# Down and output products of a split-float32 transformer kernel: two products merged into one stream of 512 columns

## The reference

```python
for l in range(DEPTH):                       # first block
    h = h + 0.5 * swiglu(rmsnorm(h, g0), ...)
    h = h + mixer(rmsnorm(h, g1), ...)       # ... return y @ w_out
    h = h + 0.5 * swiglu(rmsnorm(h, g2), ...)  # (silu(x@w_gate)*(x@w_up)) @ w_down
for l in range(DEPTH):                       # second block
    ...
    x = x + g1 * (merged @ w_out[l])
    h2 = rms_norm(x, ln2_g[l]) * (1.0 + sc2) + sh2
    x = x + g2 * (jnp.square(jax.nn.relu(h2 @ w_ff1[l])) @ w_ff2[l])
```

## Time and profile before

| | |
|---|---|
| median of 3 runs | 1894.01 us (1892.62 to 1894.32) |
| the profiled execution's own time | 1892.72 us |
| its span in the trace | 1891.4 us |
| PE busy | 1863.0 us, 98% of the span, 15225 matmuls |
| DVE busy | 1348.1 us, 71% |
| ACT busy | 1045.7 us, 55% |
| the chain that ended last | PE 94%, DVE 3%, ACT 2% |

### The profile page before, as it was taken

The page is one execution under the profiler, slowest core; times in us unless marked ns, Lnnn a source line. Parts: engine busy times, 40 slices in busy tenths (PEclk is TensorE's granted clock), DMA queues, the critical chain, the costliest instruction groups (busy, mean ns, idle before and its releaser), DMA issues.

```text
span 1891.4 us, 36376 instructions
## 1 busy us (share of the span) xinstructions
PE 1863.0 (98%) x15225; PEld 1821.5 (96%) x15225; DVE 1348.1 (71%) x2298; ACT 1045.7 (55%) x1764; POOL 1.3 (0%) x8
## 2 busy tenths in 40 slices
PE   7999999999999999999999999999999999999998
PEld 6999998899999999999889999999999999999998
DVE  5777666577776777667658777698877558787744
ACT  6444575655444544456566544576566457656643
POOL 0000000000000000000000000000000000000000
PEclk9999999999999999999999999999999999999999
DMA  6777343346786577733334878445455554455553
GB/s 245 275 260 267 120 137 110 108 161 221 262 295 221 177 261 269 267 124 129 112 118 173 301 268 300 159 158 170 164 193 184 180 176 169 160 175 182 187 190 112
DMA packets 51810, 365.91 MB, mean 193 GB/s; under 512 B 6620, under 2 KB 8060, under 8 KB 9920
## 3 DMA queue, kind: packets, MB, share of 16 engines
q1 hardware_dynamic: 51648, 363.59, 54.5%
HBM read 362.52 MB, written 1.05 MB: 192 GB/s over the span
## 4 chain that ended last, share of the span: by engine, by line
PE 94%; DVE 3%; ACT 2%; issue 1%; DMA 0%; SPq 0%; DVEq 0%; ACTq 0%
PE bank L441 28%; PE bank L442 27%; PE bank L443 27%; PE bank L477 2%; PE bank L473 1%; PE bank L474 1%; DVE w_lo L1541 1%; PE bank L712 1%; PE bank L640 1%; ACT w_hi L1022 1%; DVE full L1583 1%; PE bank L697 0%; PE bank L742 0%; PE bank L646 0%; DVE xn_lo L1547 0%
## 5 line engine op out<-in xcount | busy, mean ns | idle before, releaser
L441 PE MATMUL bank<-xn_hi,w_hi 128*128 128x272 f32 (+2 forms) x2624 | 758.8, 289 | 1.0 <-DVE w_lo L1541 1.0
L443 PE MATMUL bank<-xn_lo,w_hi 128*128 128x272 f32 (+2 forms) x2624 | 746.0, 284 | 0.0
L442 PE MATMUL bank<-xn_hi,w_lo 128*128 128x272 f32 (+2 forms) x2624 | 746.0, 284 | 0.0
L441 PEld LDWEIGHTS bank<-xn_hi,w_hi 128*128 128x128 f32 x2624 | 494.1, 188 | 8.9 <-issue 5.9
L442 PEld LDWEIGHTS bank<-xn_hi,w_lo 128*128 128x128 f32 x2624 | 494.0, 188 | 1.1
L443 PEld LDWEIGHTS bank<-xn_lo,w_hi 128*128 128x128 f32 x2624 | 494.8, 189 | 0.0
L1541 DVE TENSOR_TENSOR w_lo<-raw_b,w_hi 128x1024 fp32r<-128x1024 f32 (+1 forms) x282 | 356.6, 1265 | 145.6 <-ACT w_hi L1022 145.1
L1541 DVE TENSOR_TENSOR w_lo<-raw_a,w_hi 128x1024 fp32r<-128x1024 f32 (+1 forms) x282 | 356.3, 1265 | 140.7 <-ACT w_hi L1022 139.7
L1022 ACT ACTIVATE w_hi<-raw_a 128x1024 fp32r<-128x1024 f32 (+1 forms) x282 | 307.0, 1090 | 260.5 <-PE bank L443 221.9
L1022 ACT ACTIVATE w_hi<-raw_b 128x1024 fp32r<-128x1024 f32 (+1 forms) x282 | 306.9, 1089 | 250.3 <-PE bank L443 225.7
L441 PE MATMUL bank<-h_hi,w_hi 128*128 128x272 f32 (+1 forms) x704 | 201.8, 287 | 0.0
(11 more groups left out here) (322 smaller groups left out, 2718.3 us busy)
## 6 DMA issues: line engine op xcount, KB each, us to landing
raw_a<-in_weights SPq DMA_DIRECT2D x123, 1024.0 KB, 4.8
raw_b<-in_weights SPq DMA_DIRECT2D x123, 1024.0 KB, 4.8
ada_raw<-in_ada_w SPq DMA_DIRECT2D x48, 1024.0 KB, 4.9
raw_a<-in_weights SPq DMA_DIRECT2D x16, 1408.0 KB, 5.9
raw_b<-in_weights SPq DMA_DIRECT2D x16, 1408.0 KB, 5.9
c_rows<-in_c_rows SPq DMA_DIRECT2D x3, 512.0 KB, 3.7
raw_a<-in_weights SPq DMA_DIRECT2D x2, 768.0 KB, 4.1
raw_b<-in_weights SPq DMA_DIRECT2D x2, 768.0 KB, 4.2
```

The lines of the kernel that those rows point to most:

```text
L441: pe.matmul(o, wh, xh, start=start, stop=False)
L442: pe.matmul(o, wl, xh, start=False, stop=False)
L443: return pe.matmul(o, wh, xl, start=False, stop=stop)
```

## The change

Where 256 token columns are live, the high and the low activations of one group are read as one moving operand of 2 x 256 columns (`pair`), in a matmul by the high weights that fills a whole bank: `wh*xh` in its columns 0 to 255 and `wh*xl` in columns 256 to 511. The product by the low weights goes to the first half. Both halves are added to `x` by DVE, one after the other. This is done in the last down product of the first block (176 products), the output of its second mixer (64), the outputs of both mixers of the second block (128) and both `w_ff2` (512): 880 products and 48 output tiles. The other stages keep three matmuls. For the pair to be one operand, a high and its low tile are now two parts of one allocation.

```diff
-            return sb(name + "_hi", [P, tiles, width], F32R, 256, 0), sb(name + "_lo", [P, tiles, width], F32R, 256, 128)
+            n = tiles * width
+            part = (n + 31) // 64 * 64 + 32
+            both = sb(name, [P, 2, part], F32R, 256, 0)
+            hi, lo = (both[:, i, 0:n].rearrange("p (k t) -> p k t", k=tiles) for i in range(2))
+            return hi, lo, lambda kk, cols: both[:, :, kk * width + cols.start:kk * width + cols.stop]
...
+    def product_apart(b, wh, wl, pair, start, stop):
+
+        pe.matmul(bank[b][:, 0:2 * N], wh, pair, start=start, stop=False, skip_group_check=True)
+        return pe.matmul(bank[b][:, 0:N], wl, pair[:, 0, :], start=False, stop=stop, skip_group_check=True)
...
+    def tiles_apart_as_ready(u, b0, pair, stage):
...
+        for kk in range(KD):
+            pe.wait_ge(*k.at("x_lo", (*stage, kk)))
+            s = slice(kk * P, (kk + 1) * P)
+            for b, (wh, wl) in enumerate((wa, wb)):
+                m = product_apart(b0 + b, wh[:, s], wl[:, s], pair(kk, TN), kk == 0, kk == KD - 1)
...
-                            m = product(bank[b][:, 0:N], wh[:, s], wl[:, s], c.f_hi[:, kf, :], c.f_lo[:, kf, :], kf == 0, kf == KF2 - 1)
+                            m = product_apart(b, wh[:, s], wl[:, s], c.f_pair(kf, TN), kf == 0, kf == KF2 - 1)
...
+                if live == TB:
+                    dve.tensor_tensor(c.x[:, m, live], c.x[:, m, live], bank[m % 4][:, N:2 * N], ALU.add).then_inc(*k.up("tile_v"))
+                    dve.wait_ge(*k.newest("tile_v"))
                 dve.tensor_tensor(c.x[:, m, live], c.x[:, m, live], bank[m % 4][:, packed(live)], ALU.add).then_inc(*k.up("tile_v", ("res", l, m)))
...
-                dve.scalar_tensor_tensor(out=c.x[:, m, TB], in0=bank[m % 4][:, 0:N], scalar=c.mod_all[:, l, 16 + m:17 + m], in1=c.x[:, m, TB],
-                                         op0=ALU.mult, op1=ALU.add).then_inc(*k.up("tile_v", ("res2", l, m)))
+                for half in (slice(N, 2 * N), TN):
+                    dve.scalar_tensor_tensor(out=c.x[:, m, TB], in0=bank[m % 4][:, half], scalar=c.mod_all[:, l, 16 + m:17 + m], in1=c.x[:, m, TB],
+                                             op0=ALU.mult, op1=ALU.add).then_inc(*k.up("tile_v", ("res2", l, m) if half == TN else None))
+                    if half != TN:
+                        dve.wait_ge(*k.newest("tile_v"))
```

More of the change, by code:

```diff
@@ L251, in __init__ @@
         place = shared
-        self.y_hi, self.y_lo = streamed("y", KD)
+        self.y_hi, self.y_lo, self.y_pair = streamed("y", KD)
         place = block_start
         shared = place
-        self.f_hi, self.f_lo = streamed("f", KF2, N)
+        self.f_hi, self.f_lo, self.f_pair = streamed("f", KF2, N)
         place = shared
@@ L269, in __init__ @@
         self.cq, self.ckv = self.cq_x[:, :, TN], self.ckv_x[:, :, TN]
[L270 to L271 removed]
+        self.cq_hi, self.cq_lo, _ = streamed("cq", 3, N)
+        self.ckv_hi, self.ckv_lo, _ = streamed("ckv", 2, N)
         self.k_rot = sb("k_rot", [96, N])
@@ L505, in leading_units, with tile_apart @@
                 tile(u + i, i, TX, c.xn_hi, c.xn_lo)
+    def tile_apart(u, b, pair):
+        take(b)
+        wh, wl = weights(u)
+        for kk in range(KD):
+            s = slice(kk * P, (kk + 1) * P)
+            m = product_apart(b, wh[:, s], wl[:, s], pair(kk, TN), kk == 0, kk == KD - 1)
+        end_unit(u, m)
+    def tiles_apart_as_ready(u, b0, pair, stage):
+        take(b0)
+        take(b0 + 1)
+        wa, wb = weights(u), weights(u + 1)
+        for kk in range(KD):
+            pe.wait_ge(*k.at("x_lo", (*stage, kk)))
+            s = slice(kk * P, (kk + 1) * P)
+            for b, (wh, wl) in enumerate((wa, wb)):
+                m = product_apart(b0 + b, wh[:, s], wl[:, s], pair(kk, TN), kk == 0, kk == KD - 1)
+                if kk == KD - 1:
+                    end_unit(u + b, m)
     def half_tiles(u, bs, cols, xh, xl, ready=()):
@@ L806, in mixer @@
                 if u == 42:
-                    tiles_as_ready(u0 + u, 0, packed(live), c.y_hi, c.y_lo, ("y", l))
+                    if live == TB:
+                        tiles_apart_as_ready(u0 + u, 0, c.y_pair, ("y", l))
+                    else:
+                        tiles_as_ready(u0 + u, 0, live, c.y_hi, c.y_lo, ("y", l))
                 free[u - 42] = [("tile_v", ("res", l, u - 42))]
@@ L810, in mixer @@
                 b = (u - 42) % 4
-                tile(u0 + u, b, packed(live), c.y_hi, c.y_lo)
+                if live == TB:
+                    tile_apart(u0 + u, b, c.y_pair)
+                else:
+                    tile(u0 + u, b, live, c.y_hi, c.y_lo)
                 free[b] = [("tile_v", ("res", l, u - 42))]
@@ L986, in mixer2 @@
                 if at == 39:
-                    tiles_as_ready(u, 0, TN, c.y2_hi, c.y2_lo, ("y2", l))
+                    tiles_apart_as_ready(u, 0, c.y2_pair, ("y2", l))
                 elif at > 40:
-                    tile(u, b, TN, c.y2_hi, c.y2_lo)
+                    tile_apart(u, b, c.y2_pair)
                 free[b] = [("tile_v", ("res2", l, at - 39))]
@@ L1714, in ffn @@
                     dve.wait_ge(k.sem["unit_done"], u + 1)
+                    if to == TN:
+                        dve.scalar_tensor_tensor(out=c.x[:, m, cols], in0=bank[b][:, N:2 * N], scalar=0.5, in1=c.x[:, m, cols], op0=ALU.mult,
+                                                 op1=ALU.add).then_inc(*k.up("tile_v"))
+                        dve.wait_ge(*k.newest("tile_v"))
                     dve.scalar_tensor_tensor(out=c.x[:, m, cols], in0=bank[b][:, to], scalar=0.5, in1=c.x[:, m, cols], op0=ALU.mult,
@@ L2120, in ff @@
                 dve.wait_ge(k.sem["unit_done"], u + 1)
-                dve.scalar_tensor_tensor(out=c.x[:, m, TB], in0=bank[4 + j][:, 0:N], scalar=c.mod_all[:, l, 40 + m:41 + m], in1=c.x[:, m, TB],
-                                         op0=ALU.mult, op1=ALU.add).then_inc(*k.up("tile_v", ("x2", l, m)))
+                for half in (slice(N, 2 * N), TN):
+                    dve.scalar_tensor_tensor(out=c.x[:, m, TB], in0=bank[4 + j][:, half], scalar=c.mod_all[:, l, 40 + m:41 + m], in1=c.x[:, m, TB],
+                                             op0=ALU.mult, op1=ALU.add).then_inc(*k.up("tile_v", ("x2", l, m) if half == TN else None))
+                    if half != TN:
+                        dve.wait_ge(*k.newest("tile_v"))
             if s < 31:
```

21 lines of the change are left out of this document (13 added, 8 removed).

## The result

The changed kernel takes 1903.33 us, the median of 4 runs (1901.60 to 1905.74), against 1893.97 us before (4 runs, 1892.62 to 1894.32): ratio 1.0055, 95% interval 1.0043 to 1.0067. The ratio is an estimate of its own and not the quotient of the two medians, which is 1.0049. By the medians it is 9.4 us slower; 8.4 were forecast.

A forecast was written before the change was run, and what follows sets the result against it. TensorE's stream, busy 98% of the span, plus its few waits was taken as the bound. Passages +8.9, merged matmul -2.1 and clock +1.6 give +8.4 us on 1894.01: 1902.4 us, range 1897.5 to 1907 (8 in 10).

The forecast's parts named there:

- DVE's carried lateness: Output stages: DVE's second addition per tile delays the next, so TensorE waits at the sums of squares; six passages, 8.9 us.
- A: Sum of squares after the output of the first block's second mixer: TensorE waits longer for DVE, +1.9 us.
- B: Sum of squares after the last down product: only the last tile's extra addition counts, +0.45 us.
- C: Sum of squares after the output of the second block's first mixer: lateness of DVE carried to the end, +2.9 us.
- D: Sum of squares after the first `w_ff2`: only the last tile's extra addition counts, +0.3 us.
- E: Sum of squares after the output of the second block's second mixer: lateness carried through the stage, +2.8 us.
- F: Sum of squares after the last `w_ff2`: only the last tile's extra addition counts, +0.5 us.
- The merged matmul: Down product and both `w_ff2`: one 512-column matmul for two of 256 saves 3.0 ns per product, 2.1 us over 688.
- The clock: After the new long waits the granted clock falls to 0.50; one fall expected among three waits, 1.6 us.
- weight loads set the pace: Rival for TensorE's stream: loads hide under 512 columns, a product takes 333 ns against 353, time 1889.1 us; chance 0.06.
- DVE's lateness does not reach TensorE: Rival at the passages: each costs only its last addition, 3.0 less 2.6 us, time 1894.4, no change; chance 0.09.
- the pair streams badly: Rival for the merged operand: reading two strips costs 10 ns more per product, 9 us above forecast, 1911 us; chance 0.08.

## Why the prediction was right, and where not

- **DVE's carried lateness: right, to a tenth or two.** The working gave A +1.9, B +0.45, C +2.9, D +0.3, E +2.8, F +0.5, together 8.9. Measured: 1.83, 0.46, 3.07, 0.27, 3.04, 0.52, together 9.2, and 8.9 without what arose ahead of the output stages at C and E. That the mechanism is this one is shown from both sides: taken out, the waits vanish; put into the kernel before, they appear; reduced to tile 7, C keeps 0.35 us. One sentence of the working does not fit its own sum: DVE had not caught up at tile 7. It added that tile at 1366.44, 0.88 us behind the start of TensorE's last matmul of the output, at 1365.56; at F, where it does wait for TensorE, these are 0.32 us apart (1881.86 to 1882.18). Had it caught up, part of the lateness would have been absorbed; the sum counted every tile in full, and that is what the trace shows.
- **The merged matmul: right in direction, wrong in size.** 688 products at 3.0 ns should have given 2.1 us. The down product gave 5.7 ns each, 1.0 us, and `w_ff2` 0.1 ns each, nothing: 1.0 in place of 2.1. The step that failed is "I take 3.0 ns per product": an average over two stages that behave differently. The row of 230.8 ns is met by the down product (229.3) and not by `w_ff2` (234); its suspicion about `w_ff2`'s "columns" pointed the wrong way, since there the layout costs only the pair. Part of the down product's 5.7 is not the matmul: before, some 0.1 us of its 352.6 x 176 lay in a stall at 1169 (two starts 0.14 and 0.22 us apart instead of 0.12).
- **The clock: the size right, the number of falls by luck.** One fall was expected, at 1.6 us. In the profiled execution two come, each setting TensorE back by 1.5 us, and only C's costs: A's is hidden, but for 0.17 us, behind waits for DVE that stood there before, which no step had foreseen. In the kernel with pairs in the output products alone two falls cost 1.5 us each. With two costly falls the forecast would have been 1.5 us short on this term alone.
- **Sum.** 9.2 of the passages, 1.5 of the clock, -1.0 of the stream, 0.17 behind A and -1.0 from the start of the program give the span's 8.9 us; 8.4 were forecast, the medians say 9.4. The term that was too large (the matmul's gain) and the one too small (C and E) both make the forecast short; the start of the program, which no step had and which differs between executions, makes up for part, by chance.
- **The rivals.** That weight loads set the pace would have given a product of 333 ns; it is 346.7 at best. That DVE's lateness does not reach TensorE is refuted by the waits of 2.7 us, that the pair streams badly by the kernel without additions. Of the sustained 131 ns for 512 columns (the Trainium skill, TensorE: Matmul & The Clock Gate, Back-to-back issue gap) no kernel here shows anything: with one weight load each, their 512-column matmuls of float32r are on average 229 ns apart or more in every stage.

## What to carry to other kernels

An instruction added to the engine that follows a stream tile by tile costs little where that engine idles between tiles and nearly its full length times the number of tiles where it is catching up; compare its round with the tile's time first, and the place where the next stage waits for its last tile. Merging matmuls without saving columns saved here at most 2% of the product's time, and in `w_ff2` as it was laid out nothing, so it pays only if nothing is added behind the last tile: give the extra additions to an earlier unit and another bank. DVE can hold up TensorE even where it has time to spare, through an instruction that itself waits for a DMA; put such a one behind the instruction that frees a bank.

## What was not expected of the hardware

- A matmul whose moving operand is a pair of strips of 256 float32r columns is followed by the next after 234 to 235 ns where tiles lie 1024 bytes apart (`w_ff2`, and the output ahead of C), and after 229.1 to 229.7 ns where they lie 1152 bytes apart (the down product, the output ahead of A, and `w_ff2` with the other layout), as means over the stage and with the same 512 columns. The 256-column matmul behind it takes 118.3 to 119.4 and 117.5 to 117.7 ns. At 1152 bytes the cost goes up and down from one tile to the next, 232 and 227 ns by turns in `w_ff2`; at 1024 bytes it is the same for all to half a nanosecond. The two strips lie 2080 and 8224 columns apart in the stages at 1024 bytes and 2336, 6368 and 9248 in those at 1152, so how far apart they are does not decide. Three matmuls per product cost 353.4 ns in `w_ff2` at both layouts. What about the addresses decides is open.
- The same stretch of matmuls can run at two paces, at full clock. In the last feed-forward of the first block, ahead of the down product, 950 matmuls of 256 columns follow one another after 116.67 ns in eight of the thirteen profiles and after 117.78 in five, which makes 1.05 us. The kernel with pairs in the down product and `w_ff2` alone was profiled twice, once at either pace (1042.74 to 1153.46 and 1042.36 to 1154.13). So it is not the program alone that decides, and differences of 1 us between two profiles or two medians have to be taken stage by stage.
- In the kernel before with doubled additions, `w_ff2`'s product is 351.1 ns instead of 353.4 with the same matmuls on the same operands. It was profiled once, and nothing here tells whether this belongs to the program or to the execution.
- After waits of 2.7 us the granted clock fell to 0.50 behind C in each of the three profiles that had such a wait with TensorE idle, behind E in two of three; behind A, after 2.15 to 2.17 us, in one of three. In the kernel before with doubled additions it fell behind A after 2.02 us and behind C after 2.35, and not behind E after 2.35. So in a range of 2.0 to 2.7 us the length of the wait does not decide.
- The DMA of the modulation weights ahead of the gap let the reduction start 5.4 to 5.5 us after its issue in some programs (after: 1160.84 to 1166.30) and 6.3 to 7.0 in others (before: 1159.81 to 1166.12; the kernel profiled twice: 6.6 and 7.0), 5.9 in one. What decides it is open.
